# Turning five of the eight token tiles with VectorE and a DRAM round trip instead of TensorE

## The reference, cut to what matters

```python
h = rmsnorm(x, norm_mix)
proj = einsum('bsd,dc->bsc', h, w_in)
qa, ka, va, ga, cq, ckv, kr, gb = split(proj)        # widths 512 128 128 512 384 256 32 512
q  = rmsnorm(cq,  q_a_norm)  @ w_uq                  # 384 -> 8 heads x 96
kv = rmsnorm(ckv, kv_a_norm) @ w_ukv                 # 256 -> 8 heads x 128
# then: windowed attention on qa ka va with a sink, latent attention on q, kv, kr,
# SiLU gates ga gb, x + concat(ya, yb) @ w_out, rmsnorm(.., final_norm)
```

## Time and profile before

| | |
|---|---|
| median of 3 runs | 622.36 us (620.47 to 624.5) |
| profiled execution: its own time / its span | 621.09 us / 619.1 us |
| PE, DVE, ACT, POOL busy | 98%, 72%, 58%, 51% of the span |
| DMA | 82.15 MB, mean 133 GB/s |

### The profile page before, as it was taken

One profiled execution on the slowest core, in us unless ns is written; L12 is line 12 of the kernel. 1 busy time (PEld: TensorE's weight loads), 2 busy tenths in 40 slices (PEclk: granted clock), 3 DMA queues, 4 the chain that ended last, 5 costly groups with the idle time before them and its releaser, 6 DMA issues.

```text
span 619.1 us, 9375 instructions
## 1 busy us (share of the span) xinstructions
PE 608.7 (98%) x3212; PEld 497.3 (80%) x3212; DVE 443.2 (72%) x859; ACT 359.2 (58%) x762; POOL 317.5 (51%) x303
## 2 busy tenths in 40 slices
PE   8999998999999999999999999999999999999996
PEld 7888886788888888888887777777777777888885
DVE  5775451433444439988999798989989898789684
ACT  6663131223334228877886777878787778633563
POOL 4624004404656532536537777887887789510701
PEclk9999999999999999999999999999999999999999
DMA  7654356386676720101006733224323423499043
GB/s 252 208 161 121 85 178 200 111 300 186 217 262 220 238 69 0 35 2 34 2 27 145 205 82 82 60 68 94 80 60 77 103 86 136 149 360 341 1 151 122
DMA packets 55694, 82.15 MB, mean 133 GB/s; under 512 B 6296, under 2 KB 30368, under 8 KB 55520
## 3 DMA queue, kind: packets, MB, share of 16 engines
q1 hardware_dynamic: 55488, 81.29, 42.0%
q10 hardware_dynamic: 160, 0.27, 0.1%
HBM read 49.16 MB, written 22.68 MB: 116 GB/s over the span
## 4 chain that ended last, share of the span: by engine, by line
PE 90%; DVE 3%; DMA 3%; ACT 1%; SPq 1%; issue 0%; POOL 0%; DVEq 0%; POOLq 0%; ACTq 0%
PE ps L1601 16%; PE ps L1603 16%; PE ps L1602 16%; PE ps L1878 10%; PE ps L1896 5%; PE ps L1895 5%; PE ps L1810 5%; PE ps L1815 5%; PE ps L1780 3%; PE ps L1830 2%; PE ps L1790 2%; PE ps L1767 2%; PE ps L1766 2%; PE ps L1791 1%; DMA q_nope_scratch<-stage 1%; PE ps L1613 1%
## 5 line engine op out<-in xcount | busy, mean ns | idle before, releaser
L1455 DVE TENSOR_TENSOR pT_lo<-ps,pT_hi 128x512 fp32r<-128x512 f32 x128 | 88.2, 691 | 16.5 <-ACT pT_hi L1060 16.5
L1060 ACT ACTIVATE pT_hi<-ps 128x512 fp32r<-128x512 f32 x128 | 76.0, 596 | 37.1 <-PE ps L1878 36.8
L773 POOL TENSOR_SCALAR p_b<-p_b,stat 128x1024 f32<-128x1024 f32 x64 | 71.9, 1124 | 36.1 <-DVE stat L1450 36.1
L1601 PE MATMUL ps<-hT_hi,w_hi 128*128 128x512 f32 x208 | 84.1, 404 | 0.0
L1603 PE MATMUL ps<-hT_hi,w_lo 128*128 128x512 f32 x208 | 81.4, 391 | 0.0
L1602 PE MATMUL ps<-hT_lo,w_hi 128*128 128x512 f32 x208 | 81.1, 390 | 0.0
L1878 PE MATMUL ps<-ident,p_b 128*128 128x128 f32 x512 | 78.1, 275 | 0.2 <-DVE pT_lo L1455 0.2
L1445 DVE TENSOR_REDUCE stat<-ps 128x1 f32<-128x1024 f32 x64 | 77.7, 1215 | 0.7 <-PE ps L1830 0.6
L1878 PEld LDWEIGHTS ps<-ident,p_b 128*128 128x128 f32 x512 | 60.9, 140 | 21.2 <-issue 7.4
L1049 ACT ACTIVATE p_b<-ps,stat 128x1024 f32<-128x1024 f32 x64 | 71.2, 1113 | 6.5 <-DVE stat L1445 2.9
L1895 PE MATMUL ps<-pT_hi,vB 128*128 128x512 f32 x128 | 55.4, 432 | 0.0
(11 more groups left out here) (218 smaller groups left out, 1469.8 us busy)
## 6 DMA issues: line engine op xcount, KB each, us to landing
w_raw<-w_in SPq DMA_DIRECT2D x13, 512.0 KB, 4.1
x_in<-x SPq DMA_DIRECT2D x8, 512.0 KB, 3.6
wt_raw<-w_out SPq DMA_DIRECT2D x8, 512.0 KB, 4.4
t_scratch<-wt_hi SPq DMA_DIRECT2D x16, 256.0 KB, 2.4
t_scratch<-wt_lo SPq DMA_DIRECT2D x16, 256.0 KB, 2.6
q<-q_h SPq DMA_DIRECT2D x16, 256.0 KB, 3.7
wn_raw<-w_in SPq DMA_DIRECT2D x8, 336.0 KB, 3.7
lat_scratch<-lat_b SPq DMA_DIRECT2D x32, 80.0 KB, 1.9
```

The lines of the kernel that those rows point to most:

```text
L773: nc.gpsimd.tensor_scalar(p_b[:, (U + 1) % 4, :], p_b[:, (U + 1) % 4, :], r_b[:, U % 4:U % 4 + 1], 0.5, ALU.mult, ALU.mult).then_inc(s_bp, 1)
L1060: nc.scalar.activation(pT_hi[:, 1 - G % 2, 4 * a:4 * a + 4, U % 4 * P:(U % 4 + 1) * P], ps[:, 4 + a, :].rearrange("p (k c) -> p k c", c=P) ...
L1455: nc.vector.tensor_tensor(pT_lo[at_], ps[:, 4 + a, :].rearrange("p (k c) -> p k c", c=P), f(pT_hi[at_]), ALU.subtract).then_inc(s_bTl, 1)
L1601: nc.tensor.matmul(o, a_hi, b_hi, start=first, stop=False, skip_group_check=goes_on)
```

## The change

Tiles 0 to 2 are turned by PE as before. Tiles 3 to 7 (`X_PE = 3`) are turned within 32x32 blocks by DVE into `x_blk` (4 KB a partition, two buffers), stored to DRAM by SP in four DMAs of 128 KB (runs of 1 KB), and fetched back fully turned by one DMA of 512 KB (runs of 2 KB) into the still unused second half of latT_hi and latT_lo. ACT and DVE then make hT_hi and hT_lo from there in two column halves. Buffer x_blk0 lies over `lat` (so `lat_stats(0)` waits until the stores of tiles 4 and 6 have landed), x_blk1 over the part of vA for tiles 4 to 7. The squares' unused output now goes to `lat` in place of PSUM, so `lat_hi(t - 2)` and `lat_lo(t - 2)` stand at the head of `lat_stats(t)` and `lat_norm(t)`. The natural products go round four pairs of banks, and a tile waits for the latent of tile t - 4 (it was t - 3). UP_BANK is rotated to fit. w_uq is loaded behind the trip of latent 0, w_ukv behind that of latent 7; rope_q stays ahead of it.

```diff
...
-        UP_BANK = (6, 7, 2, 3, 4, 5, 0, 1)
+        UP_BANK = (2, 3, 4, 5, 6, 7, 0, 1)
...
+        def x_turned(t):
+
+            a, r = ((latT_hi, 0), (latT_hi, 2), (latT_lo, 0), (latT_lo, 2))[(t - X_PE) % 4]
+            return f(a[:, r:r + 2, HALF:SEQ])
+
+        def x_quads(t, r):
+
+            return x_turned(t)[:, r, :].rearrange("p (q k c) -> p k q c", q=2, c=Q32)
+
+        def h_cols(a, t, r):
+
+            c = t * P + r * 2 * Q32
+            return a[:, :, c:c + 2 * Q32].rearrange("p k (q c) -> p k q c", c=Q32)
+
         def nat_banks(t):
-            return 2 + 2 * (t % 3), 3 + 2 * (t % 3)
+            return (2 + 2 * t) % 8, (3 + 2 * t) % 8
...
+            def store_x(t):
+                sp.wait_ge(s_xblk, t - X_PE + 1)
+                for q in range(4):
+                    sp.dma_start(xt_scr[t - X_PE, :, :, q, :].rearrange("a p c -> p a c"),
+                                 x_blk[t % 2][q * Q32:(q + 1) * Q32].rearrange("p a k c -> p a (k c)")) \
+                        .then_inc(s_xsto[t % 2], 16)
+
+            def fetch_x(t):
+                sp.wait_ge(s_xsto[t % 2], 64 * ((t - X_PE) // 2 + 1))
+                if t == X_PE + 4:
+                    sp.wait_ge(s_hT, 2 * (X_PE + 1))
+                sp.dma_start(x_turned(t), xt_scr[t - X_PE].rearrange("a p (r q) c -> (a p) r (q c)", r=2)) \
+                    .then_inc(s_xq[(t - X_PE) % 4], 16)
+
+            store_x(3)
             load_x(6)
+            store_x(4)
+            fetch_x(3)
             load_x(7)
-            sp.dma_start(r_nat[:, :, :, :], rope_nat).then_inc(s_rnat, 16)
-            sp.dma_start(sinkb[:, :], attn_sink.partition_broadcast(P)).then_inc(s_sink, 16)
-            sp.wait_ge(s_wnr, 2 * KT)
-            sp.dma_start(uq_raw[:, :, :, :],
-                         w_uq.rearrange("(k p) (h c) -> p k h c", p=P, c=QK)).then_inc(s_uqi, 16)
-
+            for t in range(4, NT):
+                if t < NT - 1:
+                    store_x(t + 1)
+                fetch_x(t)
+            sp.dma_start(r_nat[:, :, :, :], rope_nat).then_inc(s_small, 16)
+            sp.dma_start(sinkb[:, :], attn_sink.partition_broadcast(P)).then_inc(s_small, 16)
             def move_lat(t):
 
                 sp.wait_ge(s_lblk, t + 1)
@@ -415,11 +452,15 @@
 
             for t in range(NT - 1):
                 move_lat(t)
+                if t == 0:
+                    sp.wait_ge(s_wnr, 2 * KT)
+                    sp.dma_start(uq_raw[:, :, :, :],
+                                 w_uq.rearrange("(k p) (h c) -> p k h c", p=P, c=QK)).then_inc(s_uqi, 16)
             sp.wait_ge(s_pB, NT)
+            sp.dma_start(r_q[:, :, :], rope_q).then_inc(s_rq, 16)
+            move_lat(NT - 1)
             sp.dma_start(ukv_raw[:, :, :, :],
                          w_ukv.rearrange("(k p) (h c) -> p k h c", p=P, c=P)).then_inc(s_ukvi, 16)
-            sp.dma_start(r_q[:, :, :], rope_q).then_inc(s_rq, 16)
-            move_lat(NT - 1)
 
...
             pool.wait_ge(s_uqi, 16)
-            pool.wait_ge(s_xT, 2 * NT)
+            pool.wait_ge(s_xblk, NT - X_PE)
...
             def h_hi(t, halves=range(2)):
+                if t >= X_PE:
+                    act.wait_ge(s_xq[(t - X_PE) % 4], 16 * ((t - X_PE) // 4 + 1))
+                    for r in range(2):
+                        nc.scalar.activation(h_cols(hT_hi, t, r), x_quads(t, r), ACT.Copy).then_inc(s_hhi, 1)
+                    return
...
-                if t >= 2:
+                if t >= X_PE + 2:
+                    act.wait_ge(s_xblk, t - 1 - X_PE)
+                elif t >= 2:
...
-                if t == 2:
-                    act.wait_ge(s_hT, 2 * NT)
-                squares = lat[:, t, :] if t < 2 else ps[:, 0:2, :].rearrange("p b c -> p (b c)")
-                nc.scalar.activation(squares[:, 0:QL], ps[:, a, P:NA], ACT.Square,
+                if t >= 2:
+                    lat_hi(t - 2)
+                    act.wait_ge(s_latT, t - 1)
+                elif t == 0:
+                    act.wait_ge(s_xsto[0], 128)
+                nc.scalar.activation(lat[:, t % 2, 0:QL], ps[:, a, P:NA], ACT.Square,
                                      accum_out=lss[:, 0:1]).then_inc(s_va, 1)
                 act.wait_ge(s_pB, t + 1)
                 nc.scalar.activation(kr_n[:, t, :], ps[:, b, KVL:KVL + ROPE], ACT.Copy)
-                nc.scalar.activation(squares[:, HALF:HALF + KVL] if t >= 2 else squares[:, QL:QL + KVL],
+                nc.scalar.activation(lat[:, t % 2, QL:QL + KVL],
                                      ps[:, b, 0:KVL], ACT.Square, accum_out=lss[:, 1:2]).then_inc(s_lss, 1)
-                if t >= 2:
-                    lat_hi(t - 2)
                 act.wait_ge(s_lvar, t + 1)
                 nc.scalar.activation(lrms, lvar, ACT.Sqrt).then_inc(s_lrms, 1)
...
-            h_hi(3)
             wn_hi_k(6)
             square_x(5)
-            h_hi(4)
             wn_hi_k(7)
             square_x(6)
-            h_hi(5)
+            h_hi(3)
             square_x(7)
             lat_stats(0)
-            h_hi(6)
-            h_hi(7)
+            h_hi(4)
 
 
             for t in range(1, NT):
                 lat_stats(t)
+                if t < 4:
+                    h_hi(4 + t)
             lat_hi(NT - 2)
...
             def h_lo(t, halves=range(2)):
+                if t >= X_PE:
+                    for r in range(2):
+                        dve.wait_ge(s_hhi, 2 * t + r + 1)
+                        nc.vector.tensor_tensor(h_cols(hT_lo, t, r), x_quads(t, r), f(h_cols(hT_hi, t, r)),
+                                                ALU.subtract).then_inc(s_hT, 1)
+                    return
...
+                if t >= 2:
+                    lat_lo(t - 2)
...
-                if t >= 2:
-                    lat_lo(t - 2)
-                    dve.wait_ge(s_latT, t - 1)
...
-            for t in range(1, 4):
+            for t in range(1, 3):
                 norm_x(t)
-                if t < 3:
-                    h_lo(t)
-            for t in range(4, NT):
+                h_lo(t)
+            def turn_blocks(t):
+                dve.wait_ge(s_xn, 2 * (t + 1))
+                if t >= X_PE + 2:
+                    dve.wait_ge(s_xsto[t % 2], 64 * ((t - X_PE) // 2))
+                nc.vector.transpose(x_blk[t % 2][:, :, :, :],
+                                    x_n[:, t % 2, :].rearrange("p (k a c) -> p a k c", a=4, c=Q32)).then_inc(s_xblk, 1)
+
+            for t in range(X_PE, NT):
                 norm_x(t)
-                if t < NT - 1:
-                    h_lo(t - 1)
+                turn_blocks(t)
+                if t == 6:
+                    h_lo(3)
             lat_norm(0)
-            h_lo(NT - 2)
-            h_lo(NT - 1)
+            h_lo(4)
...
             for t in range(1, NT):
                 lat_norm(t)
+                if t < 4:
+                    h_lo(4 + t)
...
-            turn_x(3)
             for k in (4, 5):
                 for t in range(3):
                     both(t, (k,))
-                turn_x(k)
             both(0, (6, 7))
             both(1, (6, 7))
-            turn_x(6)
             both(2, (6, 7))
-            pe.wait_ge(s_hT, 2 * 4)
-            pe.wait_ge(s_lat, 1)
-            natural(3, 0, range(1))
-            turn_x(7)
             for t in range(3, NT):
+                pe.wait_ge(s_hT, 2 * (t + 1))
                 if t > 3:
-                    pe.wait_ge(s_hT, 2 * (t + 1))
-                    pe.wait_ge(s_lat, t - 2)
-                natural(t, 0, range(1 if t == 3 else 0, KT))
+                    pe.wait_ge(s_lat, t - 3)
+                natural(t, 0, range(KT))
                 natural(t, 1, range(KT))
 
             for j, (kind, t, h) in enumerate(UP):
                 o = ps[:, UP_BANK[j % 8], :]
                 cols = slice(h * HALF, (h + 1) * HALF)
                 if j == 0:
-                    pe.wait_ge(s_lat, 6)
                     pe.wait_ge(s_latT, 4)
                     pe.wait_ge(s_uq, 1)
-                elif j in (2, 4):
-                    pe.wait_ge(s_lat, 6 + j // 2)
+                if j in (0, 2, 4, 6):
+                    pe.wait_ge(s_lat, 5 + j // 2)
                 if j == 8:
                     pe.wait_ge(s_latT, NT)
                 if kind == "kr" and h == 0:
@@ -1909,7 +1960,7 @@
                     else:
...
```

More of the change, by code:

```diff
@@ L64 @@
 BASE = 16512
+X_PE = 3
 ACT_UNITS = range(2, 16, 2)
@@ L81, in encoder @@
     v_scr = nc.dram_tensor("v_scratch", [SEQ, HEADS * HD], F32, kind="Internal").ap()
+    xt_scr = nc.dram_tensor("x_turned_scratch", [NT - X_PE, 4, Q32, 4, KT * Q32], F32, kind="Internal").ap()
     lt_scr = nc.dram_tensor("lat_scratch", [NT, 4, Q32, 4, LT * Q32], F32, kind="Internal").ap()
@@ L118, in encoder @@
         latT_lo = at("latT_lo", 185, [P, LT, SEQ], F32R)
+        x_blk = [at(f"x_blk{i}", kb, [P, 4, KT, Q32]) for i, kb in enumerate((147, 161))]
         uq_raw = at("uq_raw", 115, [P, QLT, HEADS, QK])
@@ L216, in encoder @@
         s_id = sem("ident_ready")
```

(17 more changed lines are left out.)

## The result

The changed kernel takes **625.92 us** (625.3 to 627.56, 9 runs) against 621.13 (620.36 to 624.5, 9 runs) of the kernel before beside it: a ratio of **1.0079**, 95% interval 1.0064 to 1.0095. It is 0.8% slower; 618.2 had been forecast, and the range ended at 622.5. The profiled execution took 625.59 us with a span of 623.7, 4.6 more than before.

What follows compares the result with a forecast made beforehand. PE was taken to bound the kernel, with 90% of the last chain. Turns removed 4.5 us, waits at tiles 3 and 4 cost 2.6, w_ukv's move gains 1.6: 3.5 us gained, 618.2 us forecast, range 614.8 to 622.5.

Steps and rivals of the forecast that it cites:

- The five turns: PE's turns of tiles 3 to 7, no longer executed: 4.5 us taken off PE's timeline.
- Tile 3: First wait: PE wants it at 38.3, DVE's list has it ready at 40.4, so PE waits 2.1 us.
- tile 4: Second wait: statistics of latent 0 wait for tile 6's stores; ready at 49.7, wanted at 49.2, 0.5 us more.
- T: End of PE's natural products: 86.67 before, 82.2 without waits, forecast at 84.8 with them.
- the term of 1.9 us: Gain at T: five turns removed, less the waits at tiles 3 and 4; 84.8 against 86.67.
- w_uq's cover: w_uq, loaded later, lands near 60 and POOL has split it by 70; wanted at T, cover 14 us.
- The failed step: Later tiles and latents: 8.8 us of naturals per tile against 6 us per latent trip, so nothing piles up.
- its companion on w_uq: With w_uq moved, SP reaches latent 0's stores some 8 us later, which only that trip feels.
- third term: w_ukv behind latent 7: the 2.0 us wait at job 8 goes, the stage chain decides; 1.6 us gained.
- gone by then: rope_q's one MB was taken to have left the queue before latent 7's stores, which then take 3.2 us.
- The rival: Slower than before: x tile trips of 4 us make tile 4 ready at 57.3, 626.5 us; chance 0.12.
- the other rivals: No wait at tiles 3 and 4, 615.4 to 616.3 (0.20); slow 32-partition stores, 622 (0.12); w_ukv's megabyte dear, 621.4 (0.06).

Runs made afterwards that it cites:

- e9: Kernel before with only the changed kernel's order of latents (splits of latent t - 2 ahead of tile t's squares, which write into `lat`): 619.93 us, ratio 0.9969.
- e8: Kernel before, with SP waiting for tile 3's products ahead of latent 0's trip, so the trips start late: 621.51 us, ratio 1.0005.
- e10: Kernel before with both the late start of the latents' trips and the changed kernel's order of latents: 625.48 us, ratio 1.0061.
- e1: Changed kernel with the squares' unused output in its own scratch and the splits of latent t - 2 behind the squares again: 622.85 us, ratio 1.0044.
- e7: Changed kernel with e1's edit and w_uq loaded behind latent 2's trip instead of latent 0's: 621.54 us, ratio 1.0018.
- e4: Changed kernel with 56 transposes of the identity keeping PE busy ahead of its wait at job 8: 626.62 us, ratio 1.0095.
- e5: Changed kernel with w_ukv and two w_in loads issued behind the first four stage stores instead of ahead: 625.94 us, ratio 1.0073.
- e2: Changed kernel with rope_q loaded behind latent 7's trip, just ahead of w_ukv: 626.25 us, ratio 1.0094.
- e13: e7 with rope_q loaded behind latent 7's trip instead of ahead of it: 624.07 us, ratio 1.0045 against the kernel before.
- e6: Changed kernel with only w_uq moved, loaded behind latent 2's trip instead of latent 0's: 623.61 us, ratio 1.0060.

## Why the prediction was wrong

**Right, by its own steps.** The five turns went from PE's list. Tile 3 was forecast at 40.4 with 2.1 us of wait and came at 40.84 with 1.67; tile 4 at 49.7 with 0.5, and came at 50.52 with 0.67; tiles 5 to 7 did not wait; T was put at 84.8 and came at 85.69. DVE's block turn of 1024 columns, put at 1.25 us, took 1.25. ACT waited for tile 6's stores until 45.66, forecast 45. So the term of 1.9 us came out as 1.0. The two waits were no larger than forecast (2.3 us, not 2.6); PE was done with tiles 0 to 2 at 39.2 and not 38.3, for which the sum had no term (0.4 us of it stood at 25.2 already, 0.3 is one gap at 33.7), and the first matmul behind each wait steps 0.34 us and not 0.23. w_uq's cover held: POOL's split ended at 73.6 for T = 85.7, though it took 4.22 + 7.80 us and not 3.4 + 6.9.

**The failed step** is this one: "a tile's naturals last 8.8 us and a latent's trip 6, so nothing piles up", with its companion on w_uq, that the 8 us by which SP comes later to latent 0 is what "only its trip feels". It compared one trip with one tile. But the buffers couple every second latent: trip, split, squares, norm and turn of latent t lie on the way to the turn of latent t + 2. With the squares' output moved into those buffers, an edit priced at nothing, this loop takes 11.5 us for two latents at best, and took 12.9 (two of the 6.5) with the megabytes in the queue, and SP starts it 8.4 us later. PE makes two tiles in 17.5 us, so a loop that starts on time was not felt (e9), and a late start with the old order was caught up (e8). A late start of the tighter loop was felt (e10, there at a pair of banks and in latent 7's stores).

The sum then broke in its third term: latent 7 was to be turned at T + 3.4 and was at T + 9.7 (95.36); its stores took 5.3 us behind rope_q, which "gone by then" had excluded; job 8 came at T + 19.5 and not T + 13.3. The 6.3 us of late turning and the 2.1 of longer stores, less the 2.2 that the forecast had to spare, are the wait of 6.2. Against before, T to job 8 became 4.1 us longer (19.49 for 15.35); less the 1.0 gained at T that is the 3.2 by which job 8 is later. Behind it the low clock or, without that, the stage sums cost the rest of the 4.6. By the spans the third term was -5.6 us (1.0 gained at T, 4.6 lost in the end) where +1.6 was forecast. (The 20.9 us of PE from job 8 to job 20 in it are 21.0 by the earlier trace rows, which changes nothing.)

**The rival** that ended on this side had its delay in x's trips reaching tile 4. They did not; PE's loss came 55 us later, at job 8. Of the other rivals none held. The Trainium skill (SBUF — State Buffer, "Door 1: the DMA port swizzle") gives 189 GB/s, and 218 at most, for 32 partitions; from these the prediction estimated a tile's stores at 2.4 to 2.8 us, which should have made tile 3 wait 3.1; it waited 1.67. In the stretch from 30 to 40 us, with stores of three tiles in it, the DMA engines moved 326 GB/s at a share of 1.01:

```profile
30.00:40.00 10.00, 9.09 (x49) 7.46 (x47) 7.85 (x12) 3.47 (x7) 2.51 (x2) 1.00 1.01 326
```

No run isolates those stores, so the rule is not refuted, only the delay read out of it.

**What the loss is made of,** as shown: neither order nor late start alone, both together 3.8 us in the kernel before, by way of the banks and of latent 7's stores (e8 to e10); in the changed kernel 2.2 us by undoing the order (e1), 3.8 by undoing it and moving w_uq (e7), the clock and the stage stores nothing that could be measured (e4, e5). The 1.0 us that the turns leave at T is then not seen in the end, since w_uq or rope_q stands ahead of a latent or of the stage sums wherever it was put (e2, e7, e13); that last step is read from the traces of those runs, not isolated. **Open:** why equal code gave latent 0 a trip of 3.9 or 5.8 us, and what the long trips, the order and the late start cost each in the changed kernel; e1, e6 and e7 part them only within their intervals. A place for rope_q ahead of all latents wasn't tried.

## What to carry to other kernels

Work taken off a busy engine and put through DMAs in a queue that others share must be priced at the last user of the queue, not the first: follow each ring of buffers round (who frees it, how long a round lasts, how late it may start) and not one trip. A write to a scratch that nobody reads is a wait like any other: look at what its buffer waits for. A megabyte of weights less than 2 us ahead of small stores in the same queue cost them 1.5 to 6 us each time. Here it could be put behind the stores that a chain waits for only where nobody needed it soon.

## What the runs showed of the hardware

- Four stores of 80 KB went from first issue to the fetch behind them in 3.2 us with the queue free, and in 4.7 us (e4's latent 7: 96.41 to 101.13) to 9.2 us (e13's latent 3: 67.09 to 76.29) when they were issued less than 2 us behind a load of 1 to 1.2 MB. In e6 the load was issued 3.5 us ahead of latent 7's stores, and they took 3.2 again.
- DVE's 32 by 32 block turn costs 0.85 us for 640 columns and 1.25 for 1024.
- PE was idle from 99.0 to 105.18 us; its granted clock was 1.00 until 103, 0.63 in the next us and 0.50 (1.2 GHz) from 104 to 110, where it rose again. Kept busy with transposes over the same stretch it had 1.00 (2.4 GHz).
- The two halves of a tile's norm on DVE, 128 x 512 each, took 1.42 us while POOL was idle (36.55) and 2.46 (30.97) beside POOL's split of a chunk of w_in; POOL's own split of w_uq took 12.0 us in the changed kernel and 10.2 before.
